# Last branch turn, GLU and first gate turn as one stage, and softplus ahead of the weight split

## The reference

```python
q_sb, k_sb, v_sb, u_ssm, q_mem, gate_logits = split(x @ w_in[l] + b_in[l])
sb = stick_breaking_attention(q_sb, k_sb, v_sb)     # 8 heads of 128, causal
# z = q k^T * scale; log1m = log_sigmoid(-z); w = exp(log_sigmoid(z) + sum of later log1m)
y = s5(u_ssm, ...)                                  # 32 groups of 16, 64 complex states, a scan over time
g = gelu(y)
glu_a, glu_b = split(g @ ssm_w_glu[l])              # 512 -> 2 x 512
mm = softmax(q_mem k_mem^T * scale) v_mem           # 4 heads, 256 memory tokens, k and v from mem @ w_kv
gates = sigmoid(gate_logits)                        # 3 x 2048
merged = (gates[0] * (sb @ sb_w_out) + gates[1] * ((glu_a * sigmoid(glu_b)) @ ssm_w_out)
          + gates[2] * (mm @ mem_w_out))
x = layer_norm(ALPHA * x + merged @ w_o)
x = layer_norm(ALPHA * x + (silu(x @ w_gate) * (x @ w_up)) @ w_down)
```

## Time and profile before

| | |
|---|---|
| median of 3 runs | 3175.45 us (3174.64 to 3180.66) |
| the profiled execution | 3181.69 us, span 3180.0 us |
| TensorE busy | 3027.9 us (95%), 16150 matmuls |
| VectorE busy | 2062.0 us (65%) |
| ScalarE busy | 1454.3 us (46%) |
| GpSimd busy | 175.4 us (6%) |
| mean granted TensorE clock | 0.98 |
| DMA | 562.12 MB, mean 177 GB/s |

### The profile page before, as it was taken

The page is one execution under the profiler, slowest core; times in us unless marked ns, Lnnn a source line. Parts: engine busy times, 40 slices in busy tenths (PEclk is TensorE's granted clock), DMA queues, the critical chain, the costliest instruction groups (busy, mean ns, idle before and its releaser), DMA issues.

```text
span 3180.0 us, 46794 instructions
## 1 busy us (share of the span) xinstructions
PE 3027.9 (95%) x16150; PEld 2565.6 (81%) x16150; DVE 2062.0 (65%) x3161; ACT 1454.3 (46%) x1964; POOL 175.4 (6%) x218
## 2 busy tenths in 40 slices
PE   6999899999899999999989989999998999999996
PEld 5777688888788888888877777888886888888885
DVE  5888666665665655555688885666666555555556
ACT  4555454544434444444455554555534444444442
POOL 5000011110000000000000000111100000000002
PEclk8999899999999999999999999999999999999998
DMA  8545467676465555555554545676663555555553
GB/s 272 149 135 139 123 178 194 176 197 209 162 225 185 185 185 185 185 185 185 185 137 136 148 134 146 179 190 182 208 225 136 194 187 184 179 193 182 192 185 119
DMA packets 672966, 562.12 MB, mean 177 GB/s; under 512 B 20760, under 2 KB 637568, under 8 KB 671872
## 3 DMA queue, kind: packets, MB, share of 16 engines
q1 hardware_dynamic: 668688, 548.48, 56.5%
q10 hardware_dynamic: 4208, 12.74, 1.1%
HBM read 552.78 MB, written 8.39 MB: 176 GB/s over the span
## 4 chain that ended last, share of the span: by engine, by line
PE 75%; issue 9%; DVE 8%; ACT 3%; POOL 2%; DMA 1%; ACTq 1%; DVEq 0%; POOLq 0%
PE banks L1424 18%; PE banks L1411 18%; PE banks L1425 9%; PE banks L1412 9%; PE banks L1433 5%; PE banks L1435 5%; PE banks L1434 5%; DVE lo L962 3%; PE banks L1720 2%; ACT hi L638 2%; PE banks L1721 1%; DVE hh L1376 1%; DVE hh L1372 1%; ACT pt L920 1%; DVE st L1109 1%
## 5 line engine op out<-in xcount | busy, mean ns | idle before, releaser
L962 DVE TENSOR_TENSOR lo<-raw,hi 128x1024 fp32r<-128x1024 f32 x1016 | 1206.5, 1230 | 309.3 <-ACT hi L638 279.6
L638 ACT ACTIVATE hi<-raw 128x1024 fp32r<-128x1024 f32 x880 | 886.1, 1051 | 355.2 <-PE banks L1435 236.3
L1424 PE MATMUL banks<-xs,hi 128*128 128x512 f32 x2816 | 1003.0, 400 | 16.4 <-DVE lo L962 7.5
L1411 PE MATMUL banks<-xs,hi 128*128 128x512 f32 x2544 | 912.6, 402 | 2.7 <-DVE lo L962 1.4
L1425 PE MATMUL banks<-xs,lo 128*128 128x256 f32 x2816 | 792.1, 281 | 0.0
L1412 PE MATMUL banks<-xs,lo 128*128 128x256 f32 x2544 | 715.7, 281 | 0.0
L1424 PEld LDWEIGHTS banks<-xs,hi 128*128 128x128 f32 x2816 | 531.6, 189 | 153.1 <-DVE lo L962 18.5
L1411 PEld LDWEIGHTS banks<-xs,hi 128*128 128x128 f32 x2544 | 481.1, 189 | 127.4 <-issue 9.7
L1425 PEld LDWEIGHTS banks<-xs,lo 128*128 128x128 f32 x2816 | 535.0, 190 | 0.8
L1412 PEld LDWEIGHTS banks<-xs,lo 128*128 128x128 f32 x2544 | 483.5, 190 | 0.2
L1433 PE MATMUL banks<-hi,hT 128*128 128x512 f32 x704 | 276.4, 393 | 8.0 <-DVE lo L962 8.0
(11 more groups left out here) (214 smaller groups left out, 2883.1 us busy)
## 6 DMA issues: line engine op xcount, KB each, us to landing
raw<-in_ffn_w_gate_up SPq DMA_DIRECT2D x176, 1024.0 KB, 5.1
raw<-in_w_in SPq DMA_DIRECT2D x160, 1024.0 KB, 6.4
raw<-in_ffn_w_down SPq DMA_DIRECT2D x88, 1024.0 KB, 5.2
raw<-in_w_o SPq DMA_DIRECT2D x32, 1024.0 KB, 5.3
raw<-in_mem_w_kv SPq DMA_DIRECT2D x16, 1024.0 KB, 5.8
raw<-in_sb_w_out SPq DMA_DIRECT2D x32, 512.0 KB, 4.1
raw<-in_ssm_w_out SPq DMA_DIRECT2D x32, 256.0 KB, 4.5
raw<-in_mem_w_out SPq DMA_DIRECT2D x32, 256.0 KB, 4.7
```

The source lines that it names most:

```text
L638: act.activation(hi[:, hl_slot(ph, c, h), :], raw[:, slot, h * HALF:(h + 1) * HALF], ACT.Copy).then_inc(hi_ready, 1)
L962: dve.tensor_tensor(lo[:, s, :], raw[:, slot, h * HALF:(h + 1) * HALF], hi[:, s, :].bitcast(F32), ALU.subtract).then_inc(lo_ready, 1)
L1411: pe.matmul(dst[:, :], hi[:, s, w], x_t[:, k0 + k, :], start=first and k == 0, stop=False)
L1424: pe.matmul(bank[base + j], hi[:, s, w], xs[:, k, :], start=k == 0, stop=False)
```

## The change

- The first turn of the gate loop is taken out of `G` (now 15 turns, columns 1 to 15) and put with the GLU. The stage `GLU` has six chunks: gate 0 and gate 1 of column 0, the two GLU chunks, gate 2, and the branch chunk.
- TensorE makes gate 0's product where `BL` had nothing after its second score product, and the two halves of gate 1's product on either side of `y_part(2)`, `y_part(3)`, ahead of `attend(1)`. After the GLU come gate 2 and the branch chunk. GLU's tiles go to four banks (2, 3, 4, 7), and TensorE waits for takes only from the third quarter on.
- GLU's tiles are kept in `bran`, since `gate` holds the first two gates; the tanh of gates 0 and 1 stand ahead of the GLU on ScalarE, the three merges of the turn behind it on VectorE.
- SyncE loads in the new order. By the new slots `reuse_distance` of `G`'s first chunk falls from 4 to 3, that of its third rises from 3 to 4; the others stay.
- In every branch turn VectorE does `softplus(e)` ahead of its split of chunk 6 (e = 0) or 9 (e = 1) and no longer behind it; step 9 of the first pair moves behind the take of tile 4 (e = 0), and step 8 of the second pair moves ahead of softplus, step 9 behind the split (e = 1).

```diff
-    "GLU": (1, [1, 2], [4, 4]),
-    "G": (16, [0, 1, 2, 3], [1, 3, 1, 1]),
+    "GLU": (1, [0, 1, 2, 0, 1, 3], [1, 1, 4, 4, 1, 3]),
+    "G": (15, [0, 1, 2, 3], [1, 3, 1, 1]),
...
-TILES = {"U": 2, "BR": 10, "BL": 8, "GLU": 8, "G": 6, "WO": 0, "FF": 4}
+TILES = {"U": 2, "BR": 10, "BL": 8, "GLU": 14, "G": 6, "WO": 0, "FF": 4}
...
+GLU_BANK = {2: 2, 3: 3, 4: 4, 5: 7, 6: 2, 7: 3, 8: 4, 9: 7}
...
+                load_gate("GLU", 0, 0, 0, 0)
+                load_gate("GLU", 0, 0, 1, 1)
+                load_glu(2, 0)
+                load_glu(3, 1)
+                load_gate("GLU", 0, 0, 2, 4)
+                load_branches("GLU", 0, 0, 5)
+                with sp.Fori(0, 15) as i:
+                    load_gate("G", i, i + 1, 0, 0)
+                    load_branches("G", i, i + 1, 1)
+                    load_gate("G", i, i + 1, 1, 2)
+                    load_gate("G", i, i + 1, 2, 3)
...
                     if not last:
                         split(8)
+                    if last:
+                        split_next("GLU", l, 0, 0)
                     out_hi(1, S, mmT[:, bass.ds(turn, 1), 0:T])
-                    if not last:
+                    if last:
+                        first_half("GLU", l, 0, 0, bank[0], done("GLU", l, 0, 0), bias_col(l, 32))
+                        split_next("GLU", l, 0, 1)
+                    else:
                         tile(8)
                         split(9)
...
+                def gate_tanh(b, ph, i, k):
+                    act.wait_ge(tile_out, tile_no(ph, l, i, k) + (1 + TILE_CREDIT))
+                    act.activation(gate[:, b, :], gate[:, b, :], ACT.Tanh, scale=0.5).then_inc(gate_th, 1)
+
+                gate_tanh(0, "GLU", 0, 0)
+                first_half("GLU", l, 0, 1, bank[1], done("GLU", l, 0, 1), bias_col(l, 48))
+                split_next("GLU", l, 0, 2)
+                gate_tanh(1, "GLU", 0, 1)
+                for t in range(4):
+                    for k in (2 * t + 2, 2 * t + 3):
+                        first_half("GLU", l, 0, k, bank[GLU_BANK[k]], done("GLU", l, 0, 2 + t // 2, t % 2))
+                    act.wait_ge(tile_out, tile_no("GLU", l, 0, 2 * t + 3) + 1 + TILE_CREDIT)
+                    act.activation(bran[:, 1, :], bran[:, 1, :], ACT.Tanh, scale=0.5).then_inc(glu_th, 1)
+                    act.wait_ge(glu_m, 4 * l + t + 1)
+                    act.activation(ssmT[:, t, 0:T], acc[:], ACT.Copy, scale=0.5).then_inc(glu_hi, 1)
+                    if t == 1:
+                        split_next("GLU", l, 0, 3)
+                split_next("GLU", l, 0, 4)
+                first_half("GLU", l, 0, 10, bank[0], done("GLU", l, 0, 4), bias_col(l, 64))
+                gate_tanh(2, "GLU", 0, 10)
+                split_next("GLU", l, 0, 5)
+                for k in range(3):
+                    first_half("GLU", l, 0, 11 + k, bank[1 + k], done("GLU", l, 0, 5, 0 if k == 0 else 1), scale=0.5)
+
+                with act.Fori(0, 15) as i:
...
-                    scan_states(0, 8, 10)
+                    scan_states(0, 8, 9)
                     dve.wait_ge(vt_done, n * 3 + 3)
                     tile(4, v_f)
+                    scan_states(0, 9, 10)
+                    softplus(0)
                     split(5)
-                    softplus(0)
...
                     tile(7, v_f)
+                    scan_states(1, 7, 9)
+                    softplus(1)
                     if not last:
                         split(8)
-                    scan_states(1, 7, 8)
-                    softplus(1)
-                    scan_states(1, 8, 10)
+                    scan_states(1, 9, 10)
                     out_lo(1, S, part_of(mmT, turn, 1), part_of(mmT, turn, 0))
-                    if not last:
+                    if last:
+                        split_next("GLU", l, 0, 0)
+                        dve.wait_ge(merge_step, 16 * l * 5 + 5)
+                        take("GLU", l, 0, 0, bank[0], gate[:, 0, :])
+                        split_next("GLU", l, 0, 1)
+                    else:
                         dve.wait_ge(vt_done, n * 3 + 5)
...
+                take("GLU", l, 0, 1, bank[1], gate[:, 1, :])
+                split_next("GLU", l, 0, 2)
+                for t in range(4):
+                    if l + t > 0:
+                        dve.wait_ge(glu_m, 4 * l + t)
+                    for k in (2 * t + 2, 2 * t + 3):
+                        take("GLU", l, 0, k, bank[GLU_BANK[k]], bran[:, k % 2, :])
+                    dve.wait_ge(glu_th, 4 * l + t + 1)
+                    if l + t > 0:
+                        dve.wait_ge(glu_lo, 4 * l + t)
+                    dve.scalar_tensor_tensor(out=acc[:], in0=bran[:, 1, :], scalar=1.0, in1=bran[:, 0, :],
+                                             op0=ALU.add, op1=ALU.mult).then_inc(glu_m, 1)
+                    dve.wait_ge(glu_hi, 4 * l + t + 1)
+                    dve.scalar_tensor_tensor(out=ssmT[:, t, T:2 * T], in0=acc[:], scalar=0.5,
+                                             in1=ssmT[:, t, 0:T].bitcast(F32), op0=ALU.mult,
+                                             op1=ALU.subtract).then_inc(glu_lo, 1)
+                    if t == 1:
+                        split_next("GLU", l, 0, 3)
+                split_next("GLU", l, 0, 4)
+                take("GLU", l, 0, 10, bank[0], gate[:, 2, :])
+                split_next("GLU", l, 0, 5)
                 dve.wait_ge(glu_lo, 4 * l + 4)
-                with dve.Fori(0, 16) as i:
-                    n = i + 16 * l
+                for k in range(3):
+                    take("GLU", l, 0, 11 + k, bank[1 + k], bran[:, k, :], 0.5)
+                dve.wait_ge(tile_out, tile_no("GLU", l, 0, 13) + 1 + TILE_CREDIT)
+                for b in range(3):
+                    merge(b, 16 * l)
+
+                with dve.Fori(0, 15) as i:
...
                     z(1)
-                    if not last:
+                    if last:
+                        for h in range(2):
+                            product("GLU", l, 0, 0, h, bank[0], xs, 8 * h, h == 0, h == 1)
+                    else:
                         gemm(8, mT)
                     got(7)
                     pe.wait_ge(o_lo, n * 3 + 2)
                     v_turn(2, v_f, VO)
                     tri(1)
-                    if not last:
+                    if last:
+                        product("GLU", l, 0, 1, 0, bank[1], xs, 0, True, False)
+                    else:
                         half(9, xs, 0)
                     y_part(2)
                     y_part(3)
-                    if not last:
+                    if last:
+                        product("GLU", l, 0, 1, 1, bank[1], xs, 8, False, True)
+                    else:
                         half(9, xs, 1)
                     attend(1)
 
...
+                pe.wait_ge(gelu_step, (4 * l + 3) * 5 + 10)
+                pe.wait_ge(bu_copied, 16 * l + 18)
+                pe.wait_ge(w_ready, 8 * (l + 1) + 1)
+                for t in range(4):
+                    c, h = 2 + t // 2, t % 2
+                    s = hl_slot("GLU", c, h)
+                    pe.wait_ge(lo_ready, chunk_no("GLU", l, 0, c) * 2 + h + 1 + HALF_CREDIT)
+                    for ab in range(2):
+                        kk = 2 * t + 2 + ab
+                        if t > 1:
+                            pe.wait_ge(tile_out, tile_no("GLU", l, 0, kk - 4) + 1 + TILE_CREDIT)
+                        dst = bank[GLU_BANK[kk]]
+                        for k in range(4):
+                            w = slice(k * 256 + ab * P, k * 256 + (ab + 1) * P)
+                            pe.matmul(dst[:, :], hi[:, s, w], gT[:, k, :], start=k == 0, stop=False)
+                            ins = pe.matmul(dst[:, 0:T], lo[:, s, w], gT[:, k, 0:T], start=False, stop=k == 3)
+                    ins.then_inc(half_done, 1)
+                pe.wait_ge(tile_out, tile_no("GLU", l, 0, 0) + 1 + TILE_CREDIT)
+                for h in range(2):
+                    product("GLU", l, 0, 4, h, bank[0], xs, 8 * h, h == 0, h == 1)
+                pe.wait_ge(glu_lo, 4 * l + 4)
+                pe.wait_ge(o_lo, 12 * (l + 1) + 1)
+                branch_products("GLU", 0, 5, 11)
+
+                pe.wait_ge(pt_copied, 4 * (l + 1) + 1)
+                with pe.Fori(0, 15) as i:
...
```

More of the change, by code:

```diff
@@ L397, in _, with load_gate, load_glu, pieces @@
                 branch_turn("BL", 0, 3)
-                for c in range(2):
+                def load_gate(ph, i, col, b, c):
+                    load(ph, l, i, c, columns(w_in[l], (col + (3 * SBW + SSMW + MEMW + b * D) // P) * P))
+                def load_glu(c, two):
                     gv = w_glu[l].rearrange("(k p) (ab t n) -> t p k ab n", p=P, ab=2, n=P)
-                    def pieces(r, c=c, gv=gv):
+                    def pieces(r):
                         rr = r.rearrange("p (t k ab n) -> p t k ab n", t=2, k=4, ab=2)
-                        return [(rr[:, t, :, ab], gv[2 * c + t][:, :, ab]) for t in range(2) for ab in range(2)]
```

(29 more changed lines are left out.)

94 lines of the change are left out of this document (28 added, 66 removed).

## The result

The changed kernel takes 3101.92 us (median; 3096.14 to 3112.91), the kernel before beside it on the same chip 3177.76 us: ratio 0.9767, interval 0.9747 to 0.9787, so 75.8 us less. Two more sets of timings, on other occasions, gave 3173.48 to 3105.22 and 3174.34 to 3104.74: 68.3 and 69.6 us less. The forecast was 3113 in a range of 3100 to 3138, a gain of 62.7 us.

The account below looks back on a forecast made before the run. TensorE's order bounds the kernel, so time is won only where it stands still or runs slow: 35.9 - 1.0 + 29.3 - 1.5 = 62.7 us off 3175.45 gives 3113 us, range 3100 to 3138.

Parts of the forecast that it names:

- The waits of the branch turns, both heads: Six full branch turns: TensorE's waits for the masked sp_t at both heads go, 28.5 us less.
- VectorE's small slack: Branch turns: VectorE stays just ahead of TensorE, by 0.5 to 1 us at two places a turn; costed at nothing.
- Rival B: Branch turns: VectorE becomes the bound and half of the waits return, 3127 us; chance 0.12.
- GpSimd beside VectorE: Masks now run beside VectorE's splits or scan step 9 and slow them: 1 us off, bounds 0 and 7.4.
- The joined stage, 29.3 us: Second score product to gate loop: 42.2 us with one loop turn absorbed, 15.6 us less in layer 0, 13.7 in layer 1.
- (1): Joined stage, second gate chunk: TensorE waits 1.3 us for its split, which stands behind scan step 9 and memory output.
- (3): Joined stage, third gate chunk after the GLU: TensorE waits 1.1 us for the first half of its split.
- (4): Joined stage, branch chunk: TensorE waits 2.6 us for its split, which follows GLU's quarters three and four.
- The stage's clock, one in two: Joined stage: its waits pull TensorE's clock down in one layer of two, 1.5 us off, bounds 0 and 6.
- A: Rival: GLU's hand-overs set the joined stage, old waits stay and the clock drops, 15 us back, 3128 us; chance 0.20.
- C: Rival: scan steps keep VectorE's softplus late, so the reorder does nothing in branch turns, 3148 us; chance 0.04.
- D: Rival: the first gate's load lands late in each of 30 loop turns, making the kernel slower, 3238 us; chance 0.02.

Follow-up runs that it names:

- the filled wait: The kernel before, with 14 matmuls nobody reads put at TensorE's wait for the second head's mask: 3165.88 us, ratio 0.9981.
- After_third: The changed kernel itself run once more, unaltered, as the base of a later set: 3104.74 us.
- late_load: The changed kernel with the load of each loop turn's first chunk held back one more chunk: 3106.43 us beside 3104.74, ratio 0.9786.
- two_banks: The changed kernel with GLU's tiles in two banks in place of four: 3113.12 us against 3105.22.
- the two repeats: The changed kernel run twice more, unaltered, on other occasions: 3105.22 and 3104.74 us.

## Why the prediction was right, step by step

**The waits of the branch turns, both heads.** Right. All 12 are gone, and softplus alone does it. A mended head was worth its own waits and the other's stayed. One thing was missing from the price: a wait costs a little more than its idle time. In the turn at 1624.61, at clock 1.00 throughout, TensorE has 69.08 us of work around 4.72 idle; the same work takes 68.6 in the changed kernel. Six such turns make 2.5 to 3 us that the sum didn't have.

**Their clock, 5 x 1.47 = 7.4 us.** Right, and a little small. Against the turn of 73.80 us the other five lost 1.6, 1.3, 1.3, 1.5 and 2.9 us, 8.6 in all, and the filled wait brings back 8.9. So 1.47 was well read for four of them (behind the output product at 206.30 the clock is 1.00 again). The fifth, 76.7 us from start to start, lost twice as much: its clock was 0.50 from 1835.5 to 1842.2. The turns gave 39.9 us; 28.5 of waits and 8.6 to 8.9 of clock leave the 2.5 to 3 us named above. The turn's length less TensorE's work in a turn without waits would have had all three.

**VectorE's small slack.** Right that it holds, but by less than forecast. 63.30 us busy in a turn of 68.60, and TensorE shows no wait. Rival B did not come. The turn was forecast at 68.9. At the second head of four of the six turns nothing is left of the slack: the mask ends at 189.41 and the triangle product starts at 189.46 (rows below), 0.05 us behind it as in the kernel before. This costs under 0.1 us a turn: 68.60 to 68.62 us, against 68.55 and 68.53 in the two turns whose mask took 0.74. A mask any later would have been waited for, so that the slack just held is partly luck.

**GpSimd beside VectorE, 1.0 us off.** The size was right, the picture half of it. VectorE's loss is as read: a split under a mask took 2.66 us (above), a split free of it 2.36, so 0.30 us; a scan pair 0.51 us, for 0.46 in the earlier trace rows. What the prediction left out is that the mask can lose too. VectorE's, GpSimd's and TensorE's timelines of the changed kernel show both:

```profile
187.59 2.90 DVE L991 TENSOR_TENSOR lo<-raw,hi 128x1024 fp32r<-128x1024 f32 x2
187.71 1.70 POOL L617 TENSOR_TENSOR sp_t<-sp_t,causal 128x256 f32<-128x256 f32 x1 [21.65 <-DVE sp_t L1229]
189.46 0.70 PE L1641 MATMUL banks<-sp_t,ntri 128*128 128x256 f32 x2
...
299.35 0.86 DVE L1213 SCALAR_TENSOR_TENSOR scan_t<-scan,pw 128x254 f32<-128x254 f32 x2
...
324.73 1.37 DVE L1213 SCALAR_TENSOR_TENSOR scan_t<-scan,pw 128x254 f32<-128x254 f32 x2
...
324.91 0.91 POOL L617 TENSOR_TENSOR sp_t<-sp_t,causal 128x256 f32<-128x256 f32 x1 [21.64 <-DVE sp_t L1229]
...
1851.05 0.86 DVE L1213 SCALAR_TENSOR_TENSOR scan_t<-scan,pw 128x254 f32<-128x254 f32 x2
...
1851.20 2.35 POOL L617 TENSOR_TENSOR sp_t<-sp_t,causal 128x256 f32<-128x256 f32 x1 [21.66 <-DVE sp_t L1229]
```

A mask that starts ahead of the split takes 0.75 us (302.51, above). One that comes 0.12 us behind the start of a split takes 1.70, and the split 2.90. In the last turns' second heads it falls on scan step 9: at 324.91 the scan pair gives way, at 1851.20 the mask does, for 2.35 us. That is the 0.56 us for which TensorE waits in layer 1. After_third and late_load have a mask of 2.35 us and a wait of nearly 0.6 in both layers, two_banks, with masks of 0.91 and 0.92, in neither. The Trainium skill (SBUF — State Buffer, "SBUF: two separate sides") has the port pair held for a whole instruction, the other engine fully blocked; these rows agree, for both engines, with 0.54 us more for the split and about 1 us more for the mask that meets it. The mask at 1851.20 even let more than one instruction go ahead: by its end less 0.75 us (an estimate) it began its work at 1852.8, behind the scan pair and most of the four instructions that end the step. In the full turns VectorE's loss doesn't lie in TensorE's path; the mask's does, and uses up the slack.

**The joined stage, 29.3 us.** Right in kind, 27.7 + 3.7 against a forecast of 24.7 + 3.1, both with their clock. The stage took 41.21 and 42.45 us for a forecast of 42.2. The wait at (1) was 0.92 in layer 0 (forecast 1.3) and none in layer 1, where the mask came 0.56 us late instead; at (3) there was none for 1.1; at (4) 1.97 and 2.07 for 2.6; at (5) none. So 2.9 and 2.6 us for 5.0, and work of 38.31 and 39.82 us (the second partly at the low clock) for 37.0. That the stage's length came out within 1 us in layer 0 is therefore luck in part: waits forecast 2.1 us too long and work 1.3 too short set each other off. The removed turn was counted by the first of the loop, 22.27 us; a later one has 22.61.

**The stage's clock, one in two.** As costed in this profile: in layer 0 the clock stays at 1.00 behind 1.97 us, in layer 1 it falls behind 2.07. With the two repeats it fell in four stages of six. The windows of the five us behind each wait, changed kernel:

```profile
355.50:361.30 5.80, 5.75 (x33) 5.03 (x34) 4.07 (x5) 2.58 (x4) 0.00 (x0) 1.00 0.98 260
```

```profile
1881.60:1886.60 5.00, 5.00 (x20) 4.29 (x21) 3.57 (x5) 2.70 (x4) 0.00 (x0) 0.66 0.96 259
```

**Loads, nothing.** Right. Neither the change nor one chunk more of delay stops an engine in the loop.

**The rivals.** A is real at two banks (7.9 us) and kept off by four. B, C and D didn't happen: C's condition, VectorE late at softplus because of its scan steps, is refuted by 301.87 right behind the logarithm.

**The total.** 62.7 us forecast, 68.8 in the profile pair, 68 to 76 in three sets of timings. 5 us of the miss are the turns: 1.2 to 1.5 of clock, 2.5 to 3 for what a wait costs beside its idle time, and the 1.0 taken off for GpSimd, which the turns didn't pay. 3.6 are the stage and the last turns; 2.4 went the other way. The first set's median, 3101.92, lies outside of the forecast's own 3104 to 3121 and 1.9 us above the floor of the range; the other two, 3105.22 and 3104.74, lie inside.

## What to carry to other kernels

Where TensorE waits behind a light instruction of another engine, look at what stands ahead of it in that engine's queue: putting softplus ahead of a 2.4 us split that itself waited for a third engine took away 14 of 16 waits, at the price of no instruction. Ask too what the light instruction now runs beside: the mask took 0.75 us in one place and up to 2.35 in another. Price a wait with the clock behind it, read as the turn's length less the same work in a turn without the wait: the idle time alone and one slow stretch taken for all of them came out 4 us low in 40. When stages are joined, give the inner chain enough banks that its hand-overs don't become TensorE's waits, and don't count a gain of a few us as real from one stretch until the total shows it.

## What the runs showed of the hardware that was not expected

The gate loop has two paces at the same clock. Its 14 equal turns take 316.6 or 310.6 us. Both appear in one execution of the changed kernel (its second profile): layer 0's 14 turns, layer 1's, and one turn of each.

```profile
368.06:678.68 310.62, 310.62 (x1795) 273.88 (x1794) 197.16 (x267) 158.14 (x238) 41.23 (x29) 1.00 0.74 192
...
1887.73:2204.32 316.59, 316.59 (x1795) 274.61 (x1793) 196.97 (x267) 158.32 (x238) 42.48 (x29) 1.00 0.73 192
...
368.06:390.25 22.19, 22.19 (x131) 19.57 (x129) 14.77 (x20) 11.30 (x17) 3.76 (x3) 1.00 0.73 190
...
1887.73:1910.34 22.61, 22.61 (x130) 19.61 (x129) 14.65 (x20) 11.31 (x17) 3.77 (x3) 1.00 0.71 187
```

TensorE is busy without a gap and the granted clock is 1.00 in all of them, and the matmuls are the same. The starts of neighbouring matmuls of 512 and 256 columns stand 0.353 us a pair apart in the long pace and 0.347 in the short. Of 26 such loops in 13 profiled executions (the one with a matmul more left out) 11 had the long pace and 15 the short, each in kernels with the old stage and with the new, and in either layer; before had two long ones, the changed kernel's first profile two long, its repeats one long and one short each. A layer's loop is worth 6 us, so an execution can lie 12 us from another for this alone, most of the 16.8 us over which the changed kernel's single runs spread (3096.14 to 3112.91). With one more matmul the pace changed between turns and then settled at the long one. What sets it was not found.

Waits of about 3.2 us led to the low clock in five of six turns; in the kernel with the first head alone mended it was four of six, with the stage alone six of six. Of two of about 2 us in the same place one did not and one did (1.97 and 2.07 us), and in the first repeat both did, at 1.98 and 1.97. So the length of a wait alone does not decide it. The Trainium skill (TensorE: Matmul & The Clock Gate, "What's actually happening") has the clock follow how busy the engine was; the filled wait agrees, with 1.00 in both turns shown once TensorE had something to do.
